# Depthwise convolution: row copies by transfers from SyncE, and six channel chunks instead of five on TensorE

## The chip, the cores and the metric

One core of a Trainium2 chip runs the whole program. The metric is device time in microseconds, as the median of several executions. The kernel before takes 1694.37 us (three runs, 1693.78 to 1695.69).

Five engines work in parallel and meet through semaphores: TensorE (PE, with its weight loads as PEld), VectorE (DVE), ScalarE (ACT), GpSimd (POOL) and SyncE (SP), which here does nothing but issue transfers.

## The reference

Two transformer-like blocks run over 256 tokens of width 1024. The change lies in the second layer of the second block, in its convolution module:

```python
def conformer_conv(h, pw1_w, pw1_b, dw_w, dw_b, ln_g, ln_b, pw2_w, pw2_b):
    a, g = jnp.split(h @ pw1_w + pw1_b, 2, axis=-1)
    u = a * jax.nn.sigmoid(g)
    u = depthwise_conv(u, dw_w) + dw_b            # 31 taps along the tokens, each channel by itself
    u = jax.nn.silu(layernorm(u, ln_g, ln_b))
    return u @ pw2_w + pw2_b
```

Everything is float32. Before it stands a gated feed-forward layer (`ffn(0)`), behind it another (`ffn(1)`).

## The kernel before, in words

**Layout.** Activations lie with channels on the 128 partitions and 256 tokens along the free dimension. 1024 channels are eight chunks of 128, numbered 0 to 7. Every weight comes as tiles of 128x1024 (512 KB) into a ring of four slots. SyncE loads them in one fixed order (`TILES`); the load of tile n (`load`, L667) first waits until tile n - 4 has been used or split (`released`, L653). For the convolution module the order is 16 tiles `pw1` (two for each chunk: value and gate) and 8 tiles `pw2`. Most tiles are split in a high and a low part for a product of float32r operands: ACT writes the high part (L564), POOL or DVE the low part (L573), and TensorE multiplies (L840 in this stage).

**The stage.** `conv_order()` (L147) is the one list that TensorE and ScalarE both follow: eight `pw1` chunks, mixed with `rep` and `conv` entries for the chunks in `PE_CONV`, and at the end `mean`. For each chunk c:

- `pw1`: TensorE makes the two products, ACT the sigmoid (L1923, L1916), and DVE multiplies them into `upad[:, c, ...]` (`gate`, L2559), a row of 288 elements padded with zeros. The end of `gate(c)` for c of 2 and more is the event `drained(("pw1", c))`.
- The convolution itself is done in one of two ways. Chunks 0, 1 and 2 go to DVE: one `tensor_scalar` for tap 0 (L2596) and one `scalar_tensor_tensor` of 128x256 for each of 30 more taps (`convolve`, L2579 to L2587), in hardware loops over the taps. Between the loops stand the gates of the chunks from 3 on (`taps`, L2599).
- Chunks 3 to 7 (`PE_CONV`) go to TensorE. A first step makes four copies of each group b of 32 channels, shifted by r = 0 to 3 elements, so that 128 partitions hold 32 channels x 4 shifts. `replicas` on TensorE (L1344) does this with 16 products with an identity matrix into PSUM (L1353), and ACT moves the four banks to `rep` in SBUF (`replicas`, L1925, L1931). `rep` holds two chunks in turn. Then `packed_conv` (L1357) applies 32 products with prepared 128x32 blocks of `diag` (L1363) and ACT moves the result out with its bias (L1940).
- `mean`: TensorE sums all eight chunks with a matrix of ones (L1372), first those of `PE_CONV`, then, after DVE's signal `conv_sum` (L2606), those of DVE. DVE subtracts the mean (L2609), and the layer norm, the `pw2` products (L828 for the first, whose weights are not split) and the second feed-forward follow, each waiting for the one before.

**GpSimd.** During `ffn(0)` it clears `upad` (L2710) and builds the blocks of `diag`, two pieces for a chunk of `PE_CONV` (L2695): one at step f = 2, and three at each of the steps f = 19, 20 and 21. It stands in one queue with the low parts of the tiles.

**SyncE.** Its queue is a plain sequence of waits and issues. In the stage of the change it holds only the tile loads (L678); the four `pw2` tiles behind `pw1` 15 are issued as their slots come free.

Of the kernel before, what the change touches and what calls it, by code (L numbers as in the profile page):

```python
# [30 lines left out]
ACT = mybir.ActivationFunctionType  # L31
# [26 lines left out]
NF = FF // P  # L58
CONV = 31
PADL = CONV // 2  # L60
PE_CONV = (3, 4, 5, 6, 7)
TAPG = -(-CONV // 4)
REPW = T + 4 * (TAPG - 1)
UPW = REPW + 4
# [81 lines left out]

def conv_order():  # L147

    order = [("pw1", c) for c in range(PE_CONV[0] + 3)]
    for c in PE_CONV[:-1]:  # L150
        order += [("rep", c)] + ([("pw1", c + 3)] if c + 3 < KC else [])
        if c > PE_CONV[0]:
            order.append(("conv", c - 1))
    return order + [("rep", PE_CONV[-1]), ("conv", PE_CONV[-2]), ("conv", PE_CONV[-1]), ("mean", 0)]


def plan_groups():
    uq, ukv = ([(what, tb, hf) for hf in range(2) for tb in range(TB)] for what in ("uq", "ukv"))
    g = [("norm", 0), ("in", 6), ("lam",), ("in", 7), ("in", 8), ("norm", 1), ("in", 0), ("norm", 2)]
    g += uq + [("in", 1)] + ukv + [("in", 2), ("in", 3), ("in", 4), ("in", 5)]  # L160
    for i, new, one, two_, three, four in attention_rounds():
        if new is not None:
            g.append(("z", new))
        if one is not None:
            g.append(("t", one))
        if new is not None:
            g.append(("qkT", new))
        if three is not None:
            g.append(("pT", three))
        if i == H1 + 3:  # L170
            g.append(("norm", 3))
    g += [("norm", 4)] + [("wo", c) for c in range(4)]
    g += [("norm", 5)] + [("pq", c) for c in range(8)]
    g += [("ss", tb, q) for tb in range(TB) for q in range(4)]
    g += [("u", c) for c in range(UN // 2)]
    g += [("uw", c) for c in range(UN, UR)]
    g += [("rt", 0), ("rt", 1)]
    g += [("uw", c) for c in range(UR, UT)]
    for c in range(T // GB):
        g += [("g", c), ("uw", UT + c)]  # L180
    g += [("vs", q) for q in range(4)] + [("vt", q) for q in range(4)]
    g += [("norm", 6), ("q", 2), ("f", 0), ("norm", 7)]
    g += [("k", 0), ("fy", 0), ("fy", 1), ("fz", 0), ("kc", 0), ("fw", 0)]
    for c in range(1, 3):
        g += [("k", c), ("kc", c)]
    g += [("v2", "B"), ("vc", "B")]
    g += [("s2", i, c) for i in range(2 * H2) for c in range(2)]
    g += [("rt2", p) for p in range(3)] + [("eo", c) for c in range(4)]
    g.append(("norm", 8))
    g += [(x, 0, f) for f in range(NF) for x in ("fa", "fb")]  # L190
    g.append(("norm", 9))
    g += [(what, c) for what, c in conv_order() if what != "rep" and (what, c) not in (("pw1", 0), ("pw1", 1))]
    g += [("norm", 10)] + [("pw2", c) for c in range(4)]
    g.append(("norm", 11))
    g += [(x, 1, f) for f in range(NF) for x in ("fa", "fb")]
    g.append(("norm", 12))
    return g
# [101 lines left out]
def build(nc, d):  # L299

    with ExitStack() as ctx:
# [103 lines left out]
        def halves(k, dt=F32, n=16):  # L405
# [38 lines left out]
               for k, last in (("E0", "fs"), ("E1", "fg"))]  # L444
# [5 lines left out]
        fs = a3["fs"].rearrange("p (b t) -> p b t", b=2)  # L450
        fg = a3["fg"].rearrange("p (b t) -> p b t", b=2)
        a4 = cut([("up", KC * UPW), ("cv", 2048), ("cv2", 2048), ("xc", 2048), ("sig", 512),
                  ("diag", len(PE_CONV) * TAPG * P), ("rep", 2 * 4 * REPW)], base=c2n + 4096)
        upad = a4["up"].rearrange("p (c n) -> p c n", c=KC)
        cv = a4["cv"].rearrange("p (c t) -> p c t", t=T)
        cv2 = a4["cv2"].rearrange("p (c t) -> p c t", t=T)
        xc = a4["xc"].rearrange("p (c t) -> p c t", t=T)
        diag = a4["diag"].rearrange("p (c k n) -> p c k n", k=TAPG, n=P)
        rep = a4["rep"].rearrange("p (h b n) -> p h b n", h=2, b=4)
        csig = a4["sig"].rearrange("p (b t) -> p b t", b=2)  # L460


# [74 lines left out]
        gates = sem("gates")  # L537
        padded = sem("padded")
        diagonals = sem("diagonals")
        rep_made, rep_moved = sem("rep_made"), sem("rep_moved")  # L540
        ln_made = sem("ln_made")
        q_scaled = sem("q_scaled")

# [103 lines left out]
        def _(sp):  # L647
# [59 lines left out]
            for m in range(3, ADA_U):  # L707
                c = ada_after(ada_before(m))
                ada_loads[c + 7 if m < ADA_CTX + 2 else c + 6] = (m,)

            n = NS
            while n < len(TILES):
                kind = TILES[n][0]
                if n == 2 * NS:
                    for k in range(3):
                        sp.dma_start(wuq[:, k, :], d["w_uq"][k]).then_inc(latent_weights, 16)
                    for k in range(2):
                        sp.dma_start(wukv[:, k, :], d["w_ukv"][k]).then_inc(latent_weights, 16)
                if kind == "u" and TILES[n][1] == NS:

                    count = UR // NS - 1
                    sp.wait_ge(h_low, 8)
                    for m in range(3):
                        load_ada(m)
                    with sp.Fori(0, count) as it:
                        for i in range(NS):
                            load(n + i, it, NS)
                    n += NS * count
                elif kind == "u" and TILES[n][1] >= UR:

                    load(n)
                    for m in ada_loads.get(TILES[n][1], ()):
                        load_ada(m)
                    n += 1
                elif kind == "v" and TILES[n][1] == NS:

                    load_ada(ADA_U)
                    load_ada(ADA_U + 1)
                    count = J // NS - 1
                    with sp.Fori(0, count) as it:  # L740
                        load_both(n, ADA_U + 2, it)
                    n += NS * count
                elif kind == "a" and TILES[n][2] == FF_PEEL + 1:
                    with sp.Fori(0, FF_LOOPS) as it:
                        for i in range(3 * FF_UNROLL):
                            load(n + i, it, 3 * FF_UNROLL)
                    n += 3 * FF_UNROLL * FF_LOOPS
                else:
                    load(n)
                    n += 1  # L750

            for q in range(4):
# [6 lines left out]
        def _(pe):  # L759
# [581 lines left out]

            pe.wait_ge(diagonals, 2 * len(PE_CONV))

            def replicas(c):  # L1344
                n = PE_CONV.index(c)
                drained(pe, ("pw1", c))
                if n == 0:
                    pe.wait_ge(gated_raw, 2)
                for b in range(4):
                    if n:  # L1350
                        pe.wait_ge(rep_moved, 4 * (n - 1) + b + 1)
                    for r in range(4):
                        last = mm(acc[b][32 * r:32 * r + 32, 0:REPW], ident[:, 32 * b:32 * b + 32],  # L1353
                                  upad[:, c, r:r + REPW], start=True, stop=True, skip_group_check=True)
                    last.then_inc(rep_made, 1)

            def packed_conv(c):  # L1357
                n = PE_CONV.index(c)
                ps = bank(("conv", c))
                pe.wait_ge(rep_moved, 4 * (n + 1))  # L1360
                for k in range(TAPG):
                    for b in range(4):
                        last = mm(ps[32 * b:32 * b + 32, 0:T], diag[:, n, k, 32 * b:32 * b + 32],  # L1363
                                  rep[:, n % 2, b, 4 * k:4 * k + T], start=(k == 0), stop=(k == TAPG - 1),
                                  skip_group_check=True)
                fills(last, ("conv", c))

# [8 lines left out]
            for what, c in conv_order():  # L1376
# [2 lines left out]
                        raw_product(TILE_NO["pw1", 2 * c + m], acc[2 * c + m], T + 2, sums=9 if c == m == 0 else None, turn=3)  # L1379
                elif what == "pw1":  # L1380
                    split_features("pw1", c, [(("pw1", c), h_parts)], turn=4 if c == 2 else None)
                elif what == "rep":
                    replicas(c)
                elif what == "mean":
                    mean_ps = bank(("mean", 0))
                    mean_of(mean_ps, PE_CONV)
# [17 lines left out]
        def _(act):  # L1404
# [517 lines left out]
                    drained(act, ("pw1", c - 2))  # L1922
                A(csig[:, c % 2, :], ps[:, T:2 * T], ACT.Sigmoid, bias=pb[:, 2 * c + 1:2 * c + 2]).then_inc(gates, 1)  # L1923

            def replicas(c):  # L1925
                n = PE_CONV.index(c)
                if n >= 2:
                    full(act, ("conv", c - 2))
                for b in range(4):
                    act.wait_ge(rep_made, 4 * n + b + 1)  # L1930
                    A(rep[:, n % 2, b, :], acc[b][:, 0:REPW], ACT.Copy).then_inc(rep_moved, 1)  # L1931

            for what, c in conv_order():
                if what == "pw1":
                    gate_of(c)
                elif what == "rep":
                    replicas(c)
                elif what == "conv":
                    ps = full(act, ("conv", c))
                    drains(A(cv[:, c, :], ps[:, 0:T], ACT.Identity, bias=par("dw_b")[:, c:c + 1]), ("conv", c))  # L1940
# [22 lines left out]
        def _(dve):  # L1963
# [632 lines left out]
                TS(cv[:, c, :], upad[:, c, 0:T], dw[:, c * CONV:c * CONV + 1], par("dw_b")[:, c:c + 1],  # L2596
                   ALU.mult, ALU.add).then_inc(dve_step, 1)
            st.n += len(chunks)
            taps = (1, 1, 3, 5, 8, 12, CONV)  # L2599
            for i, (k0, k1) in enumerate(zip(taps, taps[1:])):  # L2600
                if k1 > k0:
                    convolve(k0, k1)
# [42 lines left out]
        def _(pool):  # L2645
# [55 lines left out]
            def ffn(layer):  # L2701
                def step(f, it=None):
# [5 lines left out]
                    if layer == 0 and it is None:  # L2708
                        if f == 2:
                            nc.gpsimd.memset(a4["up"], 0.0).then_inc(padded, 1)  # L2710
                        diagonal(1 if f == 2 else 3)

                over_ff(pool, step)

# [125 lines left out]
```

## Time and profile before

| | before |
|---|---|
| median of 3 runs | 1694.37 us (1693.78 to 1695.69) |
| span of the profiled execution | 1694.2 us |
| TensorE busy | 1657.7 us (98%) |
| VectorE busy | 1173.1 us (69%) |
| ScalarE busy | 929.3 us (55%) |
| GpSimd busy | 765.9 us (45%) |
| transfers of the SyncE queue | 309.38 MB |
| mean granted TensorE clock | 0.994 of full |
| start of the centring behind the convolution (L2609) | 1457.31 us |

The profile shows one execution. The span is the time from its first to its last instruction; it lies 0.2 us under the median of the runs, so the two are used as one number here. Times inside it are microseconds from the span's start. "Busy" means that an instruction was in work; a float32 product of 128x256 appears as two records, and records of products overlap, so that their cost is read from the distance of their starts. What stands in square brackets at the end of a line of the timeline is the idle time of the engine ahead of it and what ended it. An engine's name with q is its sequencer: SPq is SyncE's queue, where the transfers are issued.

### The profile page before, as it was taken

To read this page: it belongs to the slowest core of one execution; us is meant where nothing else is said; L and a number is where in the kernel's file an instruction comes from. 1 tells how busy PE (TensorE), PEld (TensorE's weight loads), DVE (VectorE), ACT (ScalarE), POOL (GpSimd) and SP (SyncE) were. 2 spreads that over 40 slices of the span, in tenths; PEclk is the share of its full clock that TensorE was granted. 3 is DMA by queue.
4 is the path that set the end of the run, shared out by engine and by line. 5 is a ranking of instruction groups with operands and counts; after the bars stand their busy time and mean duration, and the time that the engine had idled before them with its cause. 6 is when DMAs were issued, how large, how long until landed. Compare 5 with 4: busy or idle time off the path is not lost.

```text
span 1694.2 us, 31137 instructions
## 1 busy us (share of the span) xinstructions
PE 1657.7 (98%) x10730; PEld 1470.0 (87%) x10730; DVE 1173.1 (69%) x2096; ACT 929.3 (55%) x1523; POOL 765.9 (45%) x361
## 2 busy tenths in 40 slices
PE   8999999999999999999999999999999999999998
PEld 8778999988999998888888879958899988789997
DVE  4674289777777777778877786365655579675555
ACT  4474465587666665455454563264555564555554
POOL 4502668888999990000000014303455744235553
PEclk9999999999999999999999999999999999999999
DMA  6313565587555557888888862203555543145563
GB/s 235 102 38 120 168 210 178 183 292 258 181 177 178 168 171 260 291 286 286 290 293 286 288 227 96 97 1 125 172 186 184 184 150 119 61 153 188 186 185 123
DMA packets 86343, 312.39 MB, mean 184 GB/s; under 512 B 9842, under 2 KB 9842, under 8 KB 86130
## 3 DMA queue, kind: packets, MB, share of 16 engines
q1 hardware_dynamic: 85972, 309.38, 54.2%
q0 software_dynamic: 288, 1.97, 0.3%
q8 instruction: 44, 0.72, 0.2%
q14 instruction: 39, 0.32, 0.1%
HBM read 310.26 MB, written 1.05 MB: 184 GB/s over the span
## 4 chain that ended last, share of the span: by engine, by line
PE 84%; DVE 7%; ACT 3%; issue 3%; POOL 1%; DVEq 0%; DMA 0%; SPq 0%; ACTq 0%; POOLq 0%
PE psr L900 17%; PE psr L840 16%; PE psr L1169 10%; PE acc_all L1169 10%; PE psr L903 9%; PE acc_all L840 7%; PE psr L1116 3%; PE psr L787 1%; DVE arena L2585 1%; DVE wl L573 1%; POOL wl L573 1%; ACT wh L564 1%; PE psr L828 1%; PE psr L935 1%; PE psr L1048 1%
## 5 line engine op out<-in xcount | busy, mean ns | idle before, releaser
L573 POOL TENSOR_TENSOR wl<-ring,wh 128x1024 fp32r<-128x1024 f32 x280 | 684.0, 2445 | 548.3 <-ACT wh L564 532.0
L564 ACT ACTIVATE wh<-ring 128x1024 fp32r<-128x1024 f32 x474 | 498.9, 1054 | 307.0 <-PE psr L840 159.1
L900 PE MATMUL psr<-hb,wh 128*128 128x512 f32 x1344 | 343.5, 397 | 0.7 <-DVE hb L2002 0.7
L573 DVE TENSOR_TENSOR wl<-ring,wh 128x1024 fp32r<-128x1024 f32 x194 | 240.3, 1239 | 61.2 <-ACT wh L564 60.1
L900 PEld LDWEIGHTS psr<-hb,wh 128*128 128x128 f32 x1344 | 240.8, 189 | 45.5 <-DVE hb L2002 2.2
L840 PE MATMUL psr<-hb,wh 128*128 128x256 f32 (+1 forms) x1664 | 222.4, 286 | 5.9 <-DVE hb L1999 3.7
L840 PEld LDWEIGHTS psr<-hb,wh 128*128 128x128 f32 (+1 forms) x1664 | 209.1, 192 | 10.3 <-DVE hb L1999 4.5
L903 PEld LDWEIGHTS psr<-hb,wl 128*128 128x128 f32 x1344 | 182.7, 190 | 15.9 <-DVE wl L573 1.7
L1169 PE MATMUL psr<-wh,hb 128*128 128x512 f32 x504 | 196.1, 389 | 0.0
L1169 PE MATMUL acc_all<-wh,hb 128*128 128x512 f32 x504 | 196.1, 389 | 0.0
L903 PE MATMUL psr<-hb,wl 128*128 128x256 f32 x1344 | 187.7, 282 | 1.0 <-DVE wl L573 0.8
L2680 POOL DMA_DIRECT2D arena<-in_consts x1 | 0.8, 754 | 361.1 <-DVE x L2383 361.1
L1731 ACT ACTIVATE hb<-arena 128x256 fp32r (+1 forms) x126 | 52.7, 418 | 167.9 <-PE acc_all L1169 167.9
L840 PE MATMUL psr<-hb,wl 128*128 128x256 f32 (+1 forms) x832 | 117.8, 285 | 0.7 <-POOL wl L573 0.7
L1169 PEld LDWEIGHTS acc_all<-wh,hb 128*128 128x128 f32 x504 | 94.6, 188 | 19.7
L1169 PEld LDWEIGHTS psr<-wh,hb 128*128 128x128 f32 x504 | 94.6, 188 | 19.6
L2227 DVE SCALAR_TENSOR_TENSOR sq<-sq,acc_all 128x1024 f32<-128x1024 f32 x91 | 110.4, 1214 | 0.4
L840 PEld LDWEIGHTS psr<-hb,wl 128*128 128x128 f32 (+1 forms) x832 | 107.8, 192 | 1.2 <-POOL wl L573 1.1
L1169 PE MATMUL psr<-wl,hb 128*128 128x512 f32 x252 | 98.0, 389 | 0.0
L1169 PE MATMUL acc_all<-wl,hb 128*128 128x512 f32 x252 | 98.0, 389 | 0.0
L2529 DVE TENSOR_TENSOR fgl<-arena,fgh 128x256 fp32r<-128x256 f32 x40 | 81.3, 2032 | 21.2 <-ACT fgh L1886 21.2
L2293 DVE TENSOR_TENSOR lanes<-psr,lanes 128x256 f32<-128x256 f32 x88 | 37.3, 424 | 73.5 <-ACT lanes L1687 73.3
(375 smaller groups left out, 2709.9 us busy)
## 6 DMA issues: line engine op xcount, KB each, us to landing
ring<-in_peer_u SPq DMA_DIRECT2D x128, 512.0 KB, 3.5
ring<-in_peer_v SPq DMA_DIRECT2D x128, 512.0 KB, 5.0
sq<-in_ada_w SPq DMA_DIRECT2D x91, 512.0 KB, 4.0
ring<-in_ffn_a SPq DMA_DIRECT2D x44, 512.0 KB, 4.0
ring<-in_ffn_b SPq DMA_DIRECT2D x44, 512.0 KB, 3.4
ring<-in_ffn_d SPq DMA_DIRECT2D x44, 512.0 KB, 3.5
ring<-in_pw SPq DMA_DIRECT2D x24, 512.0 KB, 3.5
ring<-in_w_in SPq DMA_DIRECT2D x18, 512.0 KB, 3.4
```

Source lines behind the costliest of these rows:

```text
L564: nc.scalar.activation(wh[:, q % 2, :], ring[:, s, :], ACT.Copy).then_inc(high_ready, 1)
L573: eng.tensor_tensor(wl[:, q % 2, :], ring[:, n % NS, :], wh[:, q % 2, :], ALU.subtract)\
L787: last = mm(ps[:, 0:T], ones, sq[:, c * T:(c + 1) * T], start=(c == 0), stop=(c == n - 1))
L840: return mm(out, w, a, start=start, stop=stop, skip_group_check=True)
L900: mm(ps[:, :], wh[:, b, chunk(k)], hb[:, k, :, :], start=(k == 0), stop=False, skip_group_check=True)
L903: last = mm(ps[:, 0:T], wl[:, b, chunk(k)], hh[:, k, :], start=False, stop=(k == KC - 1), skip_group_check=True)
L1116: last = mm(psr[b][:, g * P:(g + 1) * P], oneA[:, i, g, :], oneB[i][:, g, :], start=True, stop=True)
L1169: last = mm(sums[2 * tb + half][:, :], act_part[:, tb * P:(tb + 1) * P], weights[:, w, half * 512:(half + 1) * 512], start=start, stop=sto ...
L1731: A(dst, part, ACT.Copy).then_inc(c_high, 1)
L2227: STT(out=w, in0=w, scalar=1.0, in1=c_rows[0], op0=ALU.mult, op1=ALU.mult, accum_out=ada[:, m, 0:1]).then_inc(ada_used, 1)
L2293: drains(TT(rights[c % 4], psr[GROUP_NO["uw", c] % NB][:, 0:T], rights[c % 4], ALU.add), ("uw", c))
L2529: TT(fgl[:, f % 2, :], fg[:, f % 2, :], fgh[:, f % 2, :], ALU.subtract).then_inc(fg_low, 1)
```

## The change

- `PE_CONV` becomes (2, 3, 4, 5, 6, 7): six chunks go to TensorE and two (0 and 1) stay on VectorE. The list `taps` gets one more entry, so that the gates of chunks 2 and 3 both come ahead of the first loop.
- `replicas` goes, on TensorE and on ScalarE. The shifted copies are made by transfers from SBUF to SBUF that SyncE issues: for each chunk 16 transfers, each of 32 partitions x 284 elements (35.5 KB), with a semaphore for each chunk. `rep` now holds all six chunks.
- These issues stand in SyncE's queue: chunk 2 behind the load of tile `pw1` 15, chunk 3 behind `pw2` 0, chunk 4 behind `pw2` 1, chunks 5, 6 and 7 behind `pw2` 3.
- `conv_order()` becomes all `pw1`, then all `conv`, then `mean`.
- GpSimd makes 12 pieces of `diag` instead of 10: three instead of one at step f = 2.
- The buffers of the stage move to the start of the arena.

```diff
-PE_CONV = (3, 4, 5, 6, 7)
+PE_CONV = (2, 3, 4, 5, 6, 7)
...
-    order = [("pw1", c) for c in range(PE_CONV[0] + 3)]
-    for c in PE_CONV[:-1]:
-        order += [("rep", c)] + ([("pw1", c + 3)] if c + 3 < KC else [])
-        if c > PE_CONV[0]:
-            order.append(("conv", c - 1))
-    return order + [("rep", PE_CONV[-1]), ("conv", PE_CONV[-2]), ("conv", PE_CONV[-1]), ("mean", 0)]
+    return [("pw1", c) for c in range(KC)] + [("conv", c) for c in PE_CONV] + [("mean", 0)]
...
+            def copies(c):
+
+                drained(sp, ("pw1", c))
+                for b in range(4):
+                    for r in range(4):
+                        sp.dma_start(rep[32 * r:32 * r + 32, PE_CONV.index(c), b, :],
+                                     upad[32 * b:32 * b + 32, c, r:r + REPW]).then_inc(copies_in[PE_CONV.index(c)], 16)
+
+            copies_behind = {TILE_NO["pw1", 15]: PE_CONV[0:1], TILE_NO["pw2", 0]: PE_CONV[1:2], TILE_NO["pw2", 1]: PE_CONV[2:3],
+                             TILE_NO["pw2", 3]: PE_CONV[3:]}
...
                     load(n)
+                    for c in copies_behind.get(n, ()):
+                        copies(c)
...
             def packed_conv(c):
                 n = PE_CONV.index(c)
                 ps = bank(("conv", c))
-                pe.wait_ge(rep_moved, 4 * (n + 1))
+                pe.wait_ge(copies_in[n], 16 * 16)
                 for k in range(TAPG):
                     for b in range(4):
                         last = mm(ps[32 * b:32 * b + 32, 0:T], diag[:, n, k, 32 * b:32 * b + 32],
-                                  rep[:, n % 2, b, 4 * k:4 * k + T], start=(k == 0), stop=(k == TAPG - 1),
+                                  rep[:, n, b, 4 * k:4 * k + T], start=(k == 0), stop=(k == TAPG - 1),
...
-            taps = (1, 1, 3, 5, 8, 12, CONV)
+            taps = (1, 1, 1, 3, 5, 8, 12, CONV)
...
-                        diagonal(1 if f == 2 else 3)
+                        diagonal(3)
```

## Rows read from the trace of the kernel before

**Rows 1.** Chain of waits through the stage: start, duration, what.
```profile
1454.73 0.87 DVE arena L2585 x2
1455.71 1.58 PE psr L1372 x6
1457.31 0.70 DVE arena L2609
```
**Rows 2.** Timeline of PE: start, duration, instruction, idle time before it.
```profile
1413.14 2.13 PE L1353 MATMUL acc_all<-arena,cst 128*32 128x284 f32 x32
1415.20 2.18 PE L840 MATMUL psr<-hb,wh 128*128 128x256 f32 x16
...
1429.14 3.66 PE L1363 MATMUL psr<-arena 128*32 128x256 f32 x64
1432.62 2.10 PE L1353 MATMUL acc_all<-arena,cst 128*32 128x284 f32 x32
1434.53 3.64 PE L1363 MATMUL psr<-arena 128*32 128x256 f32 x64
...
1452.30 2.43 PE L1372 MATMUL psr<-arena,ones 128*128 128x256 f32 x10
1455.71 1.56 PE L1372 MATMUL psr<-arena,ones 128*128 128x256 f32 x6 [0.98 <-DVEq L2606]
```
**Rows 3.** Timeline of DVE in the same stage.
```profile
1399.92 0.48 DVE L2574 SCALAR_TENSOR_TENSOR arena<-psr,prm,arena 128x256 f32<-128x256 f32 x1
...
1403.76 10.66 DVE L2585 SCALAR_TENSOR_TENSOR arena<-arena,prm 128x256 f32<-128x256 f32 x6
...
1432.95 22.64 DVE L2585 SCALAR_TENSOR_TENSOR arena<-arena,prm 128x256 f32<-128x256 f32 x57
```
**Rows 4.** Timeline of SyncE's queue: single issues, then several in a row.
```profile
1411.23 0.33 SPq L678 DMA_DIRECT2D ring<-in_pw  x1
1424.86 0.33 SPq L678 DMA_DIRECT2D ring<-in_pw  x1
1472.66 1.75 SPq L678 DMA_DIRECT2D ring<-in_pw  x4
1159.58 1.75 SPq L678 DMA_DIRECT2D ring<-in_ev_o  x4
0.76 1.82 SPq L681 DMA_DIRECT2D x<-in_x  x4
6.57 0.74 SPq L689 DMA_DIRECT2D pos_i<-in_positions  x1
7.35 0.50 SPq L690 DMA_DIRECT2D arena<-in_chunks  x1
```
**Rows 5.** Transfers by line: number, KB each, median us from issue to landing.
```profile
ring<-in_pw SPq DMA_DIRECT2D x24, 512.0 KB, 3.5
out<-sq SPq DMA_DIRECT2D x4, 256.0 KB, 2.2
```
**Rows 6.** Timeline of POOL and PE around step f = 2 of the first feed-forward.
```profile
1201.76 1.04 POOL L2695 TENSOR_TENSOR arena<-cst,prm 128x512 f32<-128x512 f32 x1
1203.47 2.68 POOL L573 TENSOR_TENSOR wl<-ring,wh 128x1024 fp32r<-128x1024 f32 x1 [0.67 <-ACT wh L564]
1362.01 4.08 POOL L2695 TENSOR_TENSOR arena<-cst,prm 128x512 f32<-128x512 f32 x3
1206.85 1.12 PE L903 MATMUL psr<-hb,wl 128*128 128x256 f32 x8
```
**Rows 7.** Stretches: length, busy PE, PEld, DVE, ACT, POOL; granted clock; transfers' share; GB/s.
```profile
1106.00:1107.00 1.00, 0.00 (x0) 0.00 (x0) 1.00 (x3) 0.69 (x3) 0.00 (x0) 1.00 0.00 0
1110.00:1111.00 1.00, 1.00 (x3) 0.51 (x4) 0.93 (x4) 0.65 (x2) 0.00 (x0) 0.50 0.00 0
1148.00:1152.00 4.00, 3.41 (x5) 1.51 (x5) 3.08 (x4) 1.26 (x2) 3.41 (x2) 0.50 0.00 0
1429.00:1452.30 23.30, 23.30 (x419) 14.07 (x418) 23.30 (x60) 7.26 (x17) 0.00 (x0) 1.00 0.01 2
```

More of the change, by code:

```diff
@@ L191, in plan_groups @@
     g.append(("norm", 9))
-    g += [(what, c) for what, c in conv_order() if what != "rep" and (what, c) not in (("pw1", 0), ("pw1", 1))]
+    g += [(what, c) for what, c in conv_order() if (what, c) not in (("pw1", 0), ("pw1", 1))]
     g += [("norm", 10)] + [("pw2", c) for c in range(4)]
@@ L452, in build @@
         a4 = cut([("up", KC * UPW), ("cv", 2048), ("cv2", 2048), ("xc", 2048), ("sig", 512),
-                  ("diag", len(PE_CONV) * TAPG * P), ("rep", 2 * 4 * REPW)], base=c2n + 4096)
+                  ("diag", len(PE_CONV) * TAPG * P), ("rep", len(PE_CONV) * 4 * REPW)])
+        assert 6 * 1024 + 2304 + 512 + len(PE_CONV) * (TAPG * P + 4 * REPW) <= 22240
         upad = a4["up"].rearrange("p (c n) -> p c n", c=KC)
@@ L458, in build @@
         diag = a4["diag"].rearrange("p (c k n) -> p c k n", k=TAPG, n=P)
-        rep = a4["rep"].rearrange("p (h b n) -> p h b n", h=2, b=4)
+        rep = a4["rep"].rearrange("p (h b n) -> p h b n", h=len(PE_CONV), b=4)
         csig = a4["sig"].rearrange("p (b t) -> p b t", b=2)
@@ L539, in build @@
         diagonals = sem("diagonals")
-        rep_made, rep_moved = sem("rep_made"), sem("rep_moved")
+        copies_in = [sem(f"copies_in{c}") for c in PE_CONV]
         ln_made = sem("ln_made")
@@ L1342, in _ @@
             pe.wait_ge(diagonals, 2 * len(PE_CONV))
[L1344 to L1355, printed above, removed]
             def packed_conv(c):
@@ L1381, in _ @@
                     split_features("pw1", c, [(("pw1", c), h_parts)], turn=4 if c == 2 else None)
-                elif what == "rep":
-                    replicas(c)
                 elif what == "mean":
@@ L1923, in gate_of @@
                 A(csig[:, c % 2, :], ps[:, T:2 * T], ACT.Sigmoid, bias=pb[:, 2 * c + 1:2 * c + 2]).then_inc(gates, 1)
[L1925 to L1931, printed above, removed]
             for what, c in conv_order():
@@ L1935, in _ @@
                     gate_of(c)
-                elif what == "rep":
-                    replicas(c)
                 elif what == "conv":
```

## The prediction

> **What bounds the kernel now.** I first read the chain of waits through the convolution, then the timelines of TensorE and VectorE beside it. The chain [rows 1] runs through VectorE's taps (L2585) to 1455.6, then through the last six records of the mean, and reaches the centring at 1457.31. So VectorE sets the end of this stage. TensorE's timeline [rows 2] shows by how little: its convolutions end at 1452.30, it sums its five chunks, sits idle for 0.98 us until VectorE's signal, and sums the other three. The two engines are balanced within one microsecond. Work must leave both, or the stage does not get shorter. Behind 1457.31 everything is serial (norm, `pw2`, feed-forward), so the start of the centring is a good marker: a shift there is a shift of the whole span. The profiled span is 1694.2 us and the median of the runs 1694.37, so a shift of the span is taken one for one as a shift of the median. A measurement of this kernel can tell about 0.2% (3.4 us) from no change.
>
> **What goes from TensorE.** One `replicas` is 32 records; from 1432.62 to the next start at 1434.53 it takes 1.91 us in the tail, and from 1413.14 to 1415.20 it takes 2.06 us between tiles [rows 2]. Five of them are 3 x 1.91 + 2 x 2.06 = 9.9 us. One `packed_conv` is 1429.14 to 1432.62, 3.48 us; one is added, +3.5. If the copies were always there, TensorE would finish the convolutions at 1452.3 - 9.9 + 3.5 = 1445.9. In that case `pw1` ends two replicas earlier: the first convolution behind it starts at 1429.14 before [rows 2], and could at 1425.0 after. The mean then runs without a pause: 8 chunks x 2 records x 0.213 us (ten records from 1452.30 in about 2.1 us) = 3.4, so the centring could start at 1449.4, 7.9 us earlier.
>
> **What goes from VectorE.** A tap costs 22.64 / 57 = 0.397 us with GpSimd idle [rows 3]. One chunk less is 31 x 0.397 = 12.3 us. While GpSimd makes low parts, VectorE is slowed far below that: six taps take 10.66 us. After the change the last loop is 38 taps (15.1 us) behind the gate of chunk 7, which can come at about 1425.5 (end of `pw1` plus 0.5 for the sigmoid). That gives 1441, and even with 5 us of further slowing it is ahead of TensorE's 1445.9. The bound leaves VectorE. ScalarE loses 20 moves, all of them beside other work: worth nothing.
>
> **What comes: 96 issues on SyncE.** This is the term that decides. SyncE's queue issues the load of `pw1` 15 at 1411.23 [rows 4]. Behind it come 16 copies, `pw2` 0, 16 copies, `pw2` 1, 16 copies, `pw2` 2 and 3, and 48 copies: 96 + 4 = 100 issues, all in one queue. Their waits are met when their turn comes: chunk 2's gate ran at 1399.92 [rows 3], the others follow with `pw1`, and `pw2` 3, the last of the four tiles, was issued at 1424.86 before [rows 4], long ahead of its turn at about 1436 now. So the last copy is issued 100 distances of an issue after 1411.23. What is this distance? A single issue shows 0.33 us. Where several stand in a row, four take 1.75 us: the first 0.33 and each further one a distance of 0.47, twice in the same way (512 KB tiles); the four loads of `x` (256 KB each) take 1.82, again 0.46 [rows 4]. The bytes make no difference. No row shows a transfer of 32 partitions. The nearest small one is L690, of 2 partitions, at 0.50 us; the 128 positions before it take 0.74. These small ones were not cheaper. I take 0.465 us, by the rows of four in a row. The lower bound is 0.28 (less than any row, allowed because a quarter of the partitions might take less), the upper 0.74 (L689).
>
> With 0.465 the last copy is issued at 1411.2 + 46.5 = 1457.7. It lands 2.2 us later, by the smallest transfer with a landing time, the output [rows 5] (3.5 for a tile as the other end; the copies are smaller than both): 1459.9. The convolution of chunk 7 follows: + 3.5 = 1463.4, the mean + 3.5 = 1466.9. Before it was 1457.3: **+9.6 us**. The earlier chunks don't matter then: chunk 5's last copy is issued at 1442.8, chunk 6's at 1450.3, and TensorE waits for each.
>
> What hangs behind these waits: TensorE's queue holds the mean behind the last convolution, and ScalarE's holds the high parts of `pw2` 2 and 3 and a table load behind its last move. Those take about 3.3 us after it and just fit beside the mean's 3.5. The tiles `pw2` 4 and later are not issued before 1472 in any case, so the copies delay no weights that are needed.
>
> **The Trainium skill against the change.** Four in a row cost 0.47 each, whatever their bytes [rows 4]. The Trainium skill, "DMA: Bandwidth & Descriptors", section "Rules for kernel authors", says to join many small transfers into one large and that under 64 KB one pays mostly overhead. The copies are 35.5 KB; by that rule they cost as much as tiles do, which is the 0.465 taken above.
>
> **TensorE's clock.** With the copies late, TensorE works 3.5 us in every 16 x 0.465 = 7.4 us from 1429 on. Two places show what happens behind gaps [rows 7]: TensorE is idle from 1106 to 1107, and the granted clock is 0.50 (1.2 instead of 2.4 GHz) at 1110; it is 0.50 again through 1148 to 1152, where TensorE was busy for 3.41 of 4 us. In this stage before, with TensorE busy throughout, it is 1.00. On the path lie the last convolution and the mean, 7 us at full clock. The cost is between 0 and 7 us. The spell from 1148 covers at least 4 us, which is 2 us lost. I take **+2.5**.
>
> **Two more pieces of `diag` at f = 2.** One piece takes 1.04 us, or 4.08 / 3 = 1.36 [rows 6]. GpSimd is free at 1202.8 before and at 1204.9 to 1205.5 after. The low part that started at 1203.47 ended at 1206.15, and its reader on TensorE started at 1206.85, a slack of 0.7. The low part now starts 1.4 to 2.0 us later, so TensorE waits 0.7 to 1.3; VectorE shares the time there with GpSimd and could add up to 1 more. I take **+1.5** (bounds 0 and 2.5). TensorE has no slack later in the feed-forward, so this stays.
>
> **Sum.** 9.6 + 2.5 + 1.5 = +13.6 us; 1694.4 + 13.6 = 1708.0.
>
> **Rivals.**
>
> 1. *The issue gets cheaper with fewer partitions, a little: 0.33 + 0.03 = 0.36 us, as the single issue shows.* The last copy is issued at 1447.2, the centring starts at 1456.4 (-0.9), and with 1.5 for GpSimd and up to 2 for the clock the time is 1695 to 1698: no change that can be told. For it: the single issue at 0.33 [rows 4]. Against it: between issues in a row there is no wait that could explain the rest. Chance 0.17.
> 2. *The other side, faster: an issue costs in proportion to its rows, and 32 take under 0.28 us.* Then all copies keep ahead of TensorE, the centring starts 7.9 us earlier and GpSimd takes 1.5 back: 1694.4 - 6.4 = 1688.0. It decides from the point where 100 issues take less than 1457.3 - 3.5 - 3.5 - 2.2 - 1411.2 = 36.9 us, less GpSimd's 1.5: an issue under 0.35 us. By the same sum a saving of 3.4 us asks for 0.32. For it: no row has 32 partitions, and all with four in a row have 128. Against: the 2-partition issue took 0.50. The Trainium skill, "Perfetto Trace Analysis", section "DMA Instruction — HWDGE (DVE, Sync)", says that the profiled duration of an issue holds the generating of all descriptors, which would make 32 rows cheaper than 128; by it this rival holds, and L690's row speaks against it. Chance 0.13.
> 3. *The issue is dearer, 0.6 to 0.74 us, as it was with many in flight at the start [rows 4], or the copies land more slowly than they are issued.* The last copy is issued at 1471 to 1485, the centring starts 23 to 37 us later: 1720 to 1735. For it: no burst of 48 issues has a counterpart before. Against: those at the start carried 256 to 512 KB each. Chance 0.12.
> 4. My forecast, an issue at 0.43 to 0.5: 1703 to 1714. Chance 0.58.
>
> **How the numbers follow.** The predicted time is that of case 4, 1708. The range must reach to no change on one side and part of case 3 on the other: 1694 to 1722. It leaves out case 2 and half of case 3. Faster by over 0.2%: 0.13, case 2 with the cheap edge of case 1. Within 0.2%: 0.17. Slower: 0.70, cases 3 and 4 with the rest.
>
> **What would show it.** In SyncE's queue of the changed kernel, 96 issues from 1411 to about 1458 at a distance of 0.465 us (0.36, 0.28 or 0.6 for the rivals). On TensorE, gaps of about 4 us ahead of the convolutions of chunks 4 to 7, ended by transfers, a granted clock of 0.5 in part of 1430 to 1465, and no idle time at the signal of VectorE. On VectorE, taps that end near 1441. At f = 2, three pieces of `diag` and a wait of 1 to 2 us on TensorE for GpSimd's low part. The prediction is wrong if the distance of the issues is under 0.4 us, or if landing takes so long that the copies and not their issue set the pace.

## The result and the profile after

The change makes the kernel slower: 1725.18 us (four runs, 1721.77 to 1727.23) against 1694.07 us (1693.42 to 1695.69). The ratio is 1.0182, with a 95% interval of 1.0169 to 1.0195: +31 us where +13.6 was forecast, and outside the range. The profiled execution is the fastest of the four, with a span of 1720.0 us, 25.8 us over the span before.

Span and measured time are not one number. In every execution for which both are on record, the measured time lies 1.6 to 1.9 us above the span. By this the profiled execution of the kernel before (1694.2) measures about 1696, an estimate from these pairs: it is 1.9 us slower than the median, and that of the changed kernel is 3.4 us faster than its own. This is the 5 us between 25.8 and 31.1.

| | before | after |
|---|---|---|
| median | 1694.07 us | 1725.18 us |
| span of the profiled execution | 1694.2 us | 1720.0 us |
| TensorE busy | 98% | 96% |
| mean granted TensorE clock | 0.994 | 0.991 |
| start of the centring (L2609, after: L2593) | 1457.31 us | 1483.17 us |

The page of the changed kernel, section 4, shows the new bound: the chain that ended last goes through SyncE's queue for 3% of the span, where it had 0% before.

```profile
PE 83%; DVE 5%; SPq 3%; ACT 3%; POOL 2%; issue 2%; DMA 0%; DVEq 0%; POOLq 0%; ACTq 0%
```

The timeline of SyncE's queue of the changed kernel (start, duration, instruction), against [rows 4]:

```profile
1408.84 0.33 SPq L674 DMA_DIRECT2D ring<-in_pw  x1
1409.21 10.12 SPq L712 DMA_DIRECT2D arena<-arena  x16
1419.37 0.58 SPq L674 DMA_DIRECT2D ring<-in_pw  x1
1419.99 10.19 SPq L712 DMA_DIRECT2D arena<-arena  x16
1430.22 0.58 SPq L674 DMA_DIRECT2D ring<-in_pw  x1
1430.85 10.00 SPq L712 DMA_DIRECT2D arena<-arena  x16
1440.89 1.05 SPq L674 DMA_DIRECT2D ring<-in_pw  x2
1441.99 31.13 SPq L712 DMA_DIRECT2D arena<-arena  x48
```

The reader is to see that the queue never rests for 64 us. Sixteen issues take 10.0 to 10.2 us and the last 48 take 31.13, one every 0.63 to 0.65 us; the forecast had 0.465. Even a tile load right behind the copies takes 0.58 us instead of 0.43. The view of the copies' line (count: shortest/median/longest in ns, first and last start) gives 591 ns as the duration of one; with the pause of 0.04 us to the next this is the distance of 0.63. The shortest, 507 ns, are three of the four copies that stand right behind a tile load:

```profile
L712 SPq DMA_DIRECT2D arena<-arena x96: 507/591/1127, 1409.2 to 1472.5; - x96
DMA to landing us min/median/max: 1.8/1.9/4.2
```

TensorE's timeline, against [rows 2]; in brackets the idle time and what ended it:

```profile
1422.13 3.66 PE L1359 MATMUL psr<-arena 128*32 128x256 f32 x64
1431.60 5.92 PE L1359 MATMUL psr<-arena 128*32 128x256 f32 x64 [5.81 <-DMA arena<-arena]
...
1463.90 5.13 PE L1359 MATMUL psr<-arena 128*32 128x256 f32 x64 [5.06 <-DMA arena<-arena]
1474.56 4.92 PE L1359 MATMUL psr<-arena 128*32 128x256 f32 x64 [5.53 <-DMA arena<-arena]
1479.42 3.72 PE L1368 MATMUL psr<-arena,ones 128*128 128x256 f32 x16
```

Five times TensorE waits for a transfer, 26.9 us in all. Behind each wait a convolution takes 4.92 to 5.92 us instead of 3.66. VectorE ends its last loop at 1440.4 and is then idle for 42.79 us, against [rows 3] (the bracket says that it then waits for TensorE's mean):

```profile
1425.15 15.23 DVE L2569 SCALAR_TENSOR_TENSOR arena<-arena,prm 128x256 f32<-128x256 f32 x38
1483.17 2.48 DVE L2593 SCALAR_TENSOR_TENSOR arena<-psr,arena 128x512 f32<-128x512 f32 x4 [42.79 <-PE psr L1368]
```

Measured from the load of `pw1` 15, which both the forecast and this execution have as a start: the last copy is issued 1472.5 - 1408.8 = 63.7 us later (46.5 forecast), its chunk's convolution starts 2.1 us after that (2.2 forecast), takes 4.9 (3.5, and 2.5 more for the clock, were forecast), and the centring starts 3.75 us after the convolution's end (3.5).

### The profile page after: what moved, and what is told of

It is laid out like the page before. It is cut to its first block, busy times and chain, and to the rows that moved or that the text cites. A ratio compares the mean times of both kernels' runs of the same rounds, so it can differ in the third digit from the quotient of the medians.

```text
span 1720.0 us, 30918 instructions
## 1 busy us (share of the span) xinstructions
PE 1654.8 (96%) x10634; PEld 1466.8 (85%) x10634; DVE 1158.5 (67%) x2065; ACT 922.5 (54%) x1504; POOL 767.5 (45%) x363
## 4 chain that ended last, share of the span: by engine, by line
PE 83%; DVE 5%; SPq 3%; ACT 3%; POOL 2%; issue 2%; DMA 0%; DVEq 0%; POOLq 0%; ACTq 0%
PE psr L909 17%; PE psr L849 17%; PE psr L1178 10%; PE acc_all L1178 10%; PE psr L912 9%; PE acc_all L849 7%; PE psr L1125 3%; SPq L712 3%; POOL wl L569 2%; PE psr L796 1%; DVE wl L569 1%; ACT wh L560 1%; PE psr L944 1%; PE psr L837 1%; PE psr L1057 1%
```

## The experiments

Theory A: an issue in SyncE's queue has a cost of its own, which does not depend on the rows or bytes that it moves, and is 0.64 us when both sides of the transfer lie in SBUF. The rivals are named with each run. In all kernels the rest of the program is as in the change, unless the text says otherwise. The diffs leave out the `.then_inc(...)` at the end of a copy, where it stays as it was, and the count of landed copies that TensorE waits for, which follows their number.

**Four transfers of 128 partitions for each chunk**, instead of 16 of 32. Does the cost go by the issue, or by rows and bytes?

```diff
-                    for r in range(4):
-                        sp.dma_start(rep[32 * r:32 * r + 32, PE_CONV.index(c), b, :],
-                                     upad[32 * b:32 * b + 32, c, r:r + REPW])
+                    sp.dma_start(rep[:, PE_CONV.index(c), b, :], upad[:, c, b:b + REPW])
```

> Each copy takes all 128 partitions, so there are 4 a chunk instead of 16 (24 in all); the bytes stay the same (3.4 MB). The channel groups are not gathered, so the convolution of chunks 2 to 7 computes something else. Theory A (an issue from SBUF to SBUF costs about 0.64 us whatever its rows): 24 + 4 issues take 18 us, all copies land before TensorE asks for them, there is no wait of TensorE for them, and the centring starts 7 to 8 us earlier than in the kernel before at an equal start of the stage: about 1687. Theory B (the cost of an issue grows with its rows, so 32 rows are already the cheap form): 24 issues at 1.5 us or more take 36 us or more, and TensorE waits: 1692 or later.

Measured: 1687.95 us, ratio 0.996 (0.9946 to 0.9974) to the kernel before. The timelines of SyncE's queue and of TensorE:

```profile
1423.65 7.96 SPq L711 DMA_DIRECT2D arena<-arena  x12
```

```profile
1425.18 20.93 PE L1358 MATMUL psr<-arena 128*32 128x256 f32 x384
```

Twelve issues of four times the rows take 7.96 us, 0.66 each, as much as an issue of 32 rows. All six convolutions run in one piece, without a wait and at full clock. The same bytes are moved in a quarter of the issues, and 37 us go away: the transfers themselves cost nothing that can be seen, their issue does. The shorter bursts ahead (2.44 to 2.53 us for four) give 0.61 to 0.63 each.

**The same 96 transfers, read from HBM.** Is it the 32 partitions, or SBUF on both sides?

```diff
-                                     upad[32 * b:32 * b + 32, c, r:r + REPW])
+                                     d["w_in"][0][32 * b:32 * b + 32, r:r + REPW])
```

> The same 96 transfers of 32 partitions x 284 elements to the same places, but read from a weight in HBM instead of from SBUF; the convolution of chunks 2 to 7 computes something else. Theory A (SBUF on both sides is what makes an issue dearer than the 0.465 us of tile loads in a row): the distance of issues falls to 0.45 to 0.48 us, the last one is issued 17 us earlier, and the time is about 1708. Theory B (32 partitions or rows of 1136 bytes are what makes it dearer, whatever the source): the distance stays 0.64 us and the time 1720 to 1727.

Measured: 1709.0 us in one run, span 1707.2. The line's own view, and the first sixteen in the timeline:

```profile
L712 SPq DMA_DIRECT2D arena<-in_w_in x96: 419/421/1462, 1412.0 to 1460.7; - x96
```

```profile
1411.97 7.40 SPq L712 DMA_DIRECT2D arena<-in_w_in  x16
```

The distance is 7.40 / 16 = 0.46 us here, the number that the forecast took from tile loads. From the load of `pw1` 15 (1411.60) to the last copy it is 49.1 us for 100 issues, 0.49 on average, with a few long ones among them. Only the source differs from the change, so SBUF on both sides is what made an issue dearer: 0.15 us on average, 0.17 in the median duration. Rows and their length are not it.

The time is also the one that was forecast (1708), but in part by luck: the issues took 2.6 us more than the forecast's 46.5, and the last convolution took 3.66 us, so that the 2.5 us for the clock were not spent.

**48 transfers of 64 partitions.** One step between 24 and 96.

```diff
-                    for r in range(4):
-                        sp.dma_start(rep[32 * r:32 * r + 32, PE_CONV.index(c), b, :],
-                                     upad[32 * b:32 * b + 32, c, r:r + REPW])
+                    for r in range(2):
+                        sp.dma_start(rep[64 * r:64 * r + 64, PE_CONV.index(c), b, :],
+                                     upad[64 * (b // 2):64 * (b // 2) + 64, c, r:r + REPW])
```

> 48 transfers of 64 partitions instead of 96 of 32, SBUF to SBUF, the same bytes; the gathered channels are the wrong ones. Theory A (a fixed cost for each issue): distance 0.62 to 0.66 us, 48 + 4 issues take 33 us, the last copy is issued at about 1442 on the clock of the changed kernel, and the time is 1690 to 1696. Theory B (a cost by rows): distance near 1.0 us or more, 52 us or more, 1708 or later.

Measured: 1691.51 us in one run, and a distance of 0.63 (5.01 us for 8) to 0.70 us (16.86 us for 24, among them one issue of 1.8 us). Theory A holds again. With half the issues the copies are almost in time: TensorE still waits 5.4 us, in three pieces.

**The copies without their shift.**

```diff
-                                     upad[32 * b:32 * b + 32, c, r:r + REPW])
+                                     upad[32 * b:32 * b + 32, c, 0:REPW])
```

> The 96 copies of the change with the source never shifted (its start is then a multiple of 64 bytes in half of the cases more); the taps inside a group of four are the wrong ones. Theory A (a fixed cost of the issue): distance 0.64 us, time 1720 to 1727 as with the change. Theory B (the shifted start costs): distance under 0.58 us and a time under 1718.

Measured: 1724.07 us in one run, median duration of an issue 591 ns, as in the change. All 16 copies of a chunk start unshifted here, against 4 in the change, so the start of the source row plays no part.

**Half of the late copies on ScalarE's queue.** Is the time spent by the queue that issues, or by something that both queues share?

```diff
             def copies(c):
+                if c >= 6:
+                    return
...
+            def act_copies(c):
+                drained(act, ("pw1", c))
+                for b in range(4):
+                    for r in range(4):
+                        act.dma_start(rep[32 * r:32 * r + 32, PE_CONV.index(c), b, :],
+                                      upad[32 * b:32 * b + 32, c, r:r + REPW]).then_inc(copies_in[PE_CONV.index(c)], 16)
...
                 elif what == "conv":
+                    if c in (2, 4):
+                        act_copies({2: 6, 4: 7}[c])
                     ps = full(act, ("conv", c))
```

> The change with the copies of chunks 6 and 7 issued by ScalarE between its other work, those of chunks 2 to 5 by SyncE as before. Theory A (each queue's sequencer spends the time of an issue): both queues keep 0.64 us an issue side by side, SyncE's last is issued at about 1452, the convolution of chunk 7 ends at about 1466, and the time is 1706 to 1713. Theory B (one generator of descriptors serves both queues and is what takes the time): the distance in each queue rises to about 1.2 us while both issue, and the time stays at 1718 or more.

Measured: 1712.34 us (two runs), ratio 1.0112 (1.0078 to 1.0146). The queues of SyncE and ScalarE while both issue:

```profile
1410.37 10.10 SPq L714 DMA_DIRECT2D arena<-arena  x16
1421.14 10.75 SPq L714 DMA_DIRECT2D arena<-arena  x16
1423.40 10.77 ACTq L1926 DMA_DIRECT2D arena<-arena  x16
1439.79 11.33 ACTq L1926 DMA_DIRECT2D arena<-arena  x16
1443.92 10.68 SPq L714 DMA_DIRECT2D arena<-arena  x16
```

Theory B had about 1.2 us an issue in each queue. The first 16 issues, alone, take 10.10 us; side by side 16 take 10.68 to 11.33. So two queues issue almost twice as much in the same time. The 6 to 12% more cannot be put down to the second queue: in the kernel with 80 copies below, a burst of 16 with no copies in another queue takes up to 10.96 us.

The last copy in SyncE's queue is issued 43.6 us after the first, against 63.3 in the change, 19.7 less. Three convolutions (12.19 us) instead of one (4.92) then stand behind it. This leaves 12.4 us, which agrees with the gain of 13 us.

**TensorE kept busy in the gaps**, with 20 products of ones ahead of each convolution from chunk 3 on.

```diff
                 ps = bank(("conv", c))
+                if n:
+                    keep_busy(20)
                 pe.wait_ge(copies_in[n], 16 * 16)
```

> The change with 20 products of ones ahead of each convolution from chunk 3 on, in the time in which TensorE waits for copies. Theory A (the convolutions of chunks 3 to 7 take 4.9 to 5.9 us instead of 3.5 because the granted clock falls in the gaps, and only the last is on the path): each takes 3.5 to 3.7 us, the span falls by 1.3 to 2.5 us against the changed kernel's, and the runs lie at 1719 to 1724. Theory B (they are slow because transfers write beside them): they stay at 4.9 us or more.

Measured: 1723.68 us (two runs), ratio 1.0179 (1.0149 to 1.0209). The last convolution with its gap, and a stretch of the changed kernel beside the same of this one (stretch and length, busy PE, PEld, DVE, ACT, POOL, granted clock, transfers' share, GB/s). Kept busy:

```profile
1470.55 4.73 PE L926 MATMUL acc_all<-ones 128*128 128x128 f32 x40
1477.73 3.66 PE L1361 MATMUL psr<-arena 128*32 128x256 f32 x64 [2.45 <-DMA arena<-arena]
```

```profile
1432.00:1438.00 6.00, 5.14 (x77) 3.52 (x78) 6.00 (x16) 0.48 (x1) 0.00 (x0) 1.00 0.49 139
```

The changed kernel:

```profile
1432.00:1438.00 6.00, 5.51 (x64) 2.79 (x56) 6.00 (x17) 0.42 (x1) 0.00 (x0) 0.65 0.44 139
```

Four of the five convolutions behind a gap take 3.66 us and the clock beside them is 1.00; one, with 3.42 us idle ahead of it, takes 5.35. So the granted clock made them slow, and not the transfers. The expected fall of the span (1.3 to 2.5 us) does not show: this execution's 96 copies took longer to issue, 65.5 us from the first to the last against 63.3. From the last copy's issue (1475.8) to the centring (1485.08) it is 9.3 us, against 10.6 in the change, so the path behind the copies is about 1.3 us shorter. The medians differ by 1.5 us, with two runs. Theory A is shown for the products and for this part of the path, and left open for the time of the kernel.

**The transfers alone: chunk 2 stays on VectorE.**

```diff
-PE_CONV = (2, 3, 4, 5, 6, 7)
+PE_CONV = (3, 4, 5, 6, 7)
...
-            taps = (1, 1, 1, 3, 5, 8, 12, CONV)
+            taps = (1, 1, 3, 5, 8, 12, CONV)
...
-                        diagonal(3)
+                        diagonal(1 if f == 2 else 3)
```

> The change with chunk 2 left on VectorE: 80 copies from SBUF to SBUF instead of 96, the transfers alone. At 0.64 us an issue the last copy is issued 84 x 0.64 = 54 us after the load of pw1 15, 10 us earlier than in the changed kernel, TensorE waits for the copies of chunks 4 to 7, and the time is 1709 to 1714. If the number of copies did not set the end, it would stay at 1720 or more.

Measured: 1713.77 us (two runs), ratio 1.0118 (1.0099 to 1.0136). With 16 copies less, the median falls by 11.4 us, against a sum of 11.6: 16 x 0.64 = 10.2, and the 1.4 us of the two pieces that are not made at f = 2. SyncE's queue in this execution:

```profile
1409.21 10.84 SPq L712 DMA_DIRECT2D arena<-arena  x16
1420.72 10.96 SPq L712 DMA_DIRECT2D arena<-arena  x16
```

These two bursts are slower than those of the change, so the last copy is issued only 9.3 us earlier, and the last convolution takes 6.06 us instead of 4.92. The centring comes 8.2 us earlier (1475.01), and the two profiled executions lie 8.1 us apart. Against the kernel before, making the copies by transfers costs 20.6 us, net of the `replicas` that go.

**The chunk alone: the kernel before with six chunks on TensorE**, its copies made by products and moves.

```diff
-PE_CONV = (3, 4, 5, 6, 7)
+PE_CONV = (2, 3, 4, 5, 6, 7)
...
-            taps = (1, 1, 3, 5, 8, 12, CONV)
+            taps = (1, 1, 1, 3, 5, 8, 12, CONV)
...
-                        diagonal(1 if f == 2 else 3)
+                        diagonal(3)
```

> The kernel before with chunk 2 on TensorE too, its copies made by products and moves as for the other chunks: the move of the chunk alone, without transfers. TensorE gets 3.5 us of convolution, 1.9 us of copies, and the sum of the mean unbroken; with 1.4 us for diag I expect 4 to 6 us more than before: 1698 to 1700. The rival, that VectorE's 12.3 us matter and it gets faster, gives 1690 or less.

Measured: 1698.1 us (nine runs), ratio 1.0031 (1.0021 to 1.004): +5.0 us. VectorE in the stage:

```profile
1462.64 2.48 DVE L2609 SCALAR_TENSOR_TENSOR arena<-psr,arena 128x512 f32<-128x512 f32 x4 [10.54 <-PE psr L1372]
```

VectorE's 12.3 us turn into 10.54 us of idle time; TensorE's added work is the whole effect: 3.5 for the convolution, 1.9 for the copies, and little else. The chunk's move pays only where TensorE gets the room.

**The version that the runs point to: through HBM.** An issue with HBM on one side is the cheap kind, and on the HBM side one transfer can gather what in SBUF lies on different partitions.

```diff
+            def put(c):
+                drained(sp, ("pw1", c))
+                sp.dma_start(d["rows"][PE_CONV.index(c)], upad[:, c, :]).then_inc(rows_out[PE_CONV.index(c)], 16)
+            def take(c):
+                n = PE_CONV.index(c)
+                sp.wait_ge(rows_out[n], 16)
+                for r in range(4):
+                    src = bass.AP(d["rows"].tensor, n * P * UPW + r, [[UPW, 32], [32 * UPW, 4], [1, REPW]])
+                    sp.dma_start(rep[32 * r:32 * r + 32, n, :, :], src).then_inc(copies_in[n], 16)
+            behind = {TILE_NO["pw1", 13]: ((put, 2), (put, 3)), TILE_NO["pw1", 14]: ((take, 2),),
+                      TILE_NO["pw1", 15]: ((put, 4), (take, 3)), TILE_NO["pw2", 1]: ((put, 5), (take, 4)),
+                      TILE_NO["pw2", 2]: ((take, 5),), TILE_NO["pw2", 3]: ((put, 6), (put, 7), (take, 6), (take, 7))}
...
```

> The whole computation. Each gated chunk is written to HBM by one transfer of 128 partitions, and read back by four, one for each shift, each of 32 partitions x 4 rows x 284 elements: 5 issues a chunk, 30 in all, none with SBUF on both sides. Theory A (only the issue on SyncE made the change slow, and it costs under 0.5 us when one side is HBM): no wait of TensorE for a copy, the centring 7 to 8 us earlier than in the kernel before at an equal start of the stage, and GpSimd's two more pieces of diag take 1.4 us back: 1687 to 1689. Theory B (the way through HBM, write, landing and read for each chunk, takes over as the bound): TensorE waits ahead of the convolutions of chunks 6 and 7, whose gates come last, and the time is 1692 or later.

Measured: 1686.55 us (five runs, 1685.25 to 1689.26) against 1693.12, ratio 0.9957 (0.9944 to 0.9971). It is faster than both kernels, by 7 us and by 39 us. The last writes and reads in SyncE's queue, and TensorE's convolutions:

```profile
1429.86 0.91 SPq L711 DMA_DIRECT2D rows<-arena  x2
1434.95 3.65 SPq L719 DMA_DIRECT2D arena<-rows  x8
```

```profile
1425.94 20.93 PE L1366 MATMUL psr<-arena 128*32 128x256 f32 x384
```

In these rows an issue costs 0.46 us each way, so neither SBUF as the source alone nor SBUF as the destination alone makes it dear. The last copies' issue ends at 1438.6, and TensorE does not wait. From the first convolution to the centring (1450.55) it takes 24.6 us; before it was 32.3, from 1425.0 (where `pw1` would end without the two `replicas` ahead of 1429.14 [rows 2]) to 1457.31. The difference of 7.7 us agrees with the 7.9 of the forecast's first part.

**The same with the pieces of `diag` placed later.**

```diff
-                        diagonal(3)
+                        diagonal({2: 1, 19: 3, 20: 4, 21: 4}[f])
```

> As e5_by_hbm, with one piece of diag at f = 2 as in the kernel before, and 3, 4 and 4 at f = 19, 20 and 21. Theory A (the two more pieces at f = 2 hold up a low part by 1.4 us, and this is never regained): 1.0 to 1.6 us less than e5_by_hbm. Theory B (they are hidden, or the four pieces at the end cost as much): no difference of more than 0.5 us.

Measured: 1686.75 us (six runs), ratio 0.9963 (0.995 to 0.9975); no difference from the version above. The waits of TensorE with three pieces at f = 2, in the version above:

```profile
1207.52 1.22 PE L919 MATMUL psr<-hb,wl 128*128 128x256 f32 x8 [1.36 <-POOL wl L570]
```

With one piece there and four at each of the last two steps:

```profile
1357.06 1.22 PE L919 MATMUL psr<-hb,wl 128*128 128x256 f32 x8 [1.16 <-POOL wl L570]
1365.68 0.39 PE L1339 MATMUL acc_all<-fgh,wh 128*128 128x256 f32 x1 [1.73 <-DVE fgl L2520]
```

The wait of 1.36 us at f = 2 goes, and two at the end grow by 1.0 and 0.8 us (0.19 and 0.90 before). The 1.4 us are real, and they only move.

## Why the prediction was wrong

- **What bounds the kernel now: right.** The sixth chunk alone made VectorE idle for 10.5 us and gained nothing; both engines had to be relieved.
- **What goes from TensorE and VectorE: right.** With copies in time, the stage is 7.7 us shorter (7.9 forecast), and VectorE ended at 1440.4 in the changed kernel (1441 forecast). The profiled execution entered the stage 2.4 us early, so this is 1442.8 on the forecast's clock, still far ahead of TensorE.
- **96 issues on SyncE: the mechanism right, the size wrong, and this is the step that failed.** The forecast took the distance of issues from tile loads in a row, 0.465 us. The copies had 0.64. Over 100 issues this is 17.2 us. The step looked at rows and bytes as what might make an issue cheaper or dearer, and was right to let neither move its value. It did not look at the one property in which no row of before resembled the copies: all of them have HBM on one side. The upper bound of 0.74 did hold it, and its rival had 1720 to 1735; it was given 0.12, and the range was cut at 1722. Read from HBM, with 0.49 on average, the kernel took 1709.0 against the 1708.0 forecast; that it is so near is in part luck, as said there.
- **Landing: right**, 1.9 us in the median (2.2).
- **TensorE's clock: right in kind, too large.** On the path it cost 4.9 - 3.5 = 1.4 us in the profiled execution (2.5 forecast). At the four convolutions ahead the cost was 1.4 to 2.3 us (5.09 to 5.92 less 3.66), hidden by the wait for the next copies. It varies: the last convolution took 3.66 us when read from HBM and 6.16 in the unshifted run, so 2.5 is the most that was seen on it.
- **Two more pieces of `diag`: right**, a wait of 1.36 us at f = 2 (1.5 forecast).
- **Rivals.** The cheap-issue rivals fell with 0.64 us for an issue of 32 rows. The Trainium skill, "Perfetto Trace Analysis", section "DMA Instruction — HWDGE (DVE, Sync)", states that the profiled duration of an issue holds the generating of its descriptors. The forecast took from it that 32 rows would be cheaper than 128; the runs show no such difference (0.64 for 32 rows, 0.66 for 128). The Trainium skill, "DMA: Bandwidth & Descriptors", section "Rules for kernel authors", has the rule to join small transfers. It agrees with the runs: from 96 transfers to 24 the time fell by 37 us. That the copies cost as much as tiles was the forecast's own reading of the rule, and the runs show 0.64 against 0.47.
- **The sum.** 13.6 + 17.2 for the issues - 1.1 for the clock, with landing, mean and `diag` nil together, gives 29.7 us. In the profiles, 28.2 of it lie between the load of `pw1` 15 and the centring (74.3 us, before 46.1), and 1.4 at f = 2. The spans show 25.8, because this execution issues the load of `pw1` 15 at 1408.84, 2.4 us earlier than the one before, for a reason ahead of the change (last section). The median moved by 31.1; the 1.4 us more than the sum are not explained. A clock that fell further in the other executions is possible (0.985 to 0.988 for the whole program, 0.991 in the profiled one), but they have no trace.

What makes an issue with SBUF on both sides dearer is not settled. The cost does not fall wholly on its own instruction: a tile load behind it takes 0.58 instead of 0.43 us, and a copy behind a tile load 0.51 instead of 0.59. It looks as if something of the earlier copy were still in work in that queue; no run tells what. What carries the bytes does not set the pace, nor does anything that both queues share, since SyncE and ScalarE together issued almost twice as many of the same copies in the same time.

## What to carry to other kernels

A queue that issues transfers is an engine with a price per issue, and moving work to it must be counted in issues, not in bytes: 96 copies of 35.5 KB took 64 us of SyncE, while the same bytes in 24 copies cost nothing visible. Before taking the price from the trace, ask in which property the new operation differs from every row there; here it was the memory on both sides, and a price that enters the sum a hundred times deserves a range as wide as its own bounds. Where a gather over partitions forces many small copies, a write to HBM and a few gathering reads can be cheaper than the direct way.

## What the runs showed of the hardware that was not expected

- An issue from SBUF to SBUF takes 0.61 to 0.70 us in a row, mostly 0.64, whether it has 32, 64 or 128 partitions; one from SBUF to HBM or back takes 0.46, or 0.49 with the long ones.
- SyncE and ScalarE issue side by side, 0.67 to 0.71 us an issue in each queue; one queue alone took 0.63 to 0.69.
- Executions of one kernel fall into groups some 3 us apart (1685.25, 1685.75 and 1686.55 against 1688.86 and 1689.26 for the version through HBM). The traces show a difference far ahead of the change: in the stretch of the `eo` products after the differential attention the granted clock is 0.81 in some executions and 1.00 in others. The kernel before, and the changed kernel (columns as above):

```profile
1144.00:1162.00 18.00, 15.70 (x63) 11.38 (x63) 9.72 (x15) 6.27 (x12) 5.28 (x2) 0.81 0.07 16
```

```profile
1144.00:1162.00 18.00, 16.54 (x95) 13.98 (x96) 9.53 (x14) 6.81 (x12) 7.06 (x3) 1.00 0.31 109
```

  TensorE waits there in both, 1.7 and 0.6 us before and 1.7 and 1.4 us in the changed kernel, so the waits alone do not decide the clock. Of the 4.1 us by which the changed kernel is ahead at the first step of the feed-forward's f = 2, 2.2 arise in this stretch and 1.9 before it. It fits that the profiled executions of the version through HBM (1689.26) and of the sixth chunk alone (1701.27) show 0.81 here, and that of the version with the pieces moved (1685.93) 1.00. That this is what parts the groups is not shown, as each kernel has one trace.

  A difference of one pair of profiled spans is therefore uncertain by about 3 us in this kernel, and the stage is best read from an event at its own start.
